# A hybrid decoder step: parameters, sample states and small state outputs cross memory channel-major instead of being transposed on the chip

## What is computed

```
u    = rmsnorm(x, norm_g);  proj = u @ w_in          # 8704 columns
lx, lg, sb, scg, sh, sg, q, qg, mg = split(proj)
# A: conv of width 4 over lx (buffer: 3 old inputs), gated linear recurrence from h0
xc, new_lru_buf = causal_dwconv(lx, lru_buf, lru_conv_w);  xc = xc + lru_conv_b
hs, new_h = rglru(xc, lru_h, lru_wa, lru_ba, lru_wx, lru_bx, lru_lambda)
z_a = (hs * silu(lg)) @ lru_wo
# B: conv of width 3 over scg * sh (buffer: 2 old inputs)
cy, new_sc_buf = causal_dwconv(scg * sh, sc_buf, sconv_w)
z_b = (silu(sg) * sb * cy) @ sconv_wo
# C: 4 heads of attention into 256 memory tokens
z_c = (attention(q, mem_k, mem_v) * silu(qg)) @ xa_wo
y = x + (sigmoid(mg_a) * z_a + sigmoid(mg_b) * z_b + sigmoid(mg_c) * z_c) @ w_out
```

## Time and profile before

| | |
|---|---|
| median of 3 runs | 780.32 us (775.95 to 801.77) |
| the profiled execution | 778.57 us |
| its spans, eight cores | 770.2 to 777.0 us |
| its granted clock, eight cores | 0.985 to 0.997 |
| span of the slowest core (core 4) | 777.0 us |
| PE busy on it | 727.6 us (94%) |
| DVE, ACT, POOL busy on it | 398.3, 344.8, 246.0 us |

### The profile page before, as it was taken

How to read it: one execution, slowest core, us unless ns; L and a number is a source line. 1 busy time by engine, 2 the same in 40 slices (tenths; PEclk the granted TensorE clock), 3 DMA queues, 4 the chain that set the end, 5 groups by cost and what they waited for, 6 DMA issues and landing times.

```text
span 777.0 us, 13244 instructions; the slowest of 8 cores (770.2 to 777.0 us)
## 1 busy us (share of the span) xinstructions
PE 727.6 (94%) x4884; PEld 459.4 (59%) x4884; DVE 398.3 (51%) x379; ACT 344.8 (44%) x408; POOL 246.0 (32%) x303
## 2 busy tenths in 40 slices
PE   2887999989999989989999999999999999999995
PEld 1555656556566546646666656666666666665442
DVE  3444253747849529727975865546321221223675
ACT  4346378687694776777661211121211112112332
POOL 5555101202103002102023344435464554523211
PEclk9999999999999989989999999999999999999998
DMA  9998934422613322412333694655895848226833
GB/s 201 187 191 148 135 72 40 41 24 19 54 17 35 34 26 28 41 11 29 38 38 72 96 182 80 101 112 65 112 111 68 109 55 74 26 109 217 288 149 139
DMA packets 112618, 69.47 MB, mean 89 GB/s; under 512 B 93987, under 2 KB 100213, under 8 KB 112539
## 3 DMA queue, kind: packets, MB, share of 16 engines
q0 software_dynamic: 99808, 31.60, 40.3%
q1 hardware_dynamic: 12747, 37.03, 14.4%
HBM read 90.53 MB, written 9.82 MB: 129 GB/s over the span
## 4 chain that ended last, share of the span: by engine, by line
PE 84%; DMA 6%; ACT 3%; DVE 2%; issue 2%; POOL 1%; POOLq 0%; SPq 0%; ACTq 0%; DVEq 0%
PE PP L644 72%; PE PP L1211 8%; DMA R<-xp 3%; DMA R<-w_in 3%; PE PP L989 2%; ACT R L847 1%; PE PP L981 1%; DVE R L834 1%; PE PP L1075 1%; ACT R L984 1%; PE PP L1114 0%; POOL R L692 0%; POOL R L702 0%; ACT R L698 0%; PE PP L770 0%
## 5 line engine op out<-in xcount | busy, mean ns | idle before, releaser
L644 PE MATMUL PP<-R 128*128 128x344 bf16 x4104 | 619.7, 311 | 7.7 <-ACT R L847 4.0
L644 PEld LDWEIGHTS PP<-R 128*128 128x128 bf16 x4104 | 399.4, 98 | 216.1 <-issue 19.4
L1163 ACT ACTIVATE R<-PP 128x688 f32<-128x688 f32 x72 | 53.5, 743 | 221.1 <-PE PP L644 188.3
L134 POOL DMA_DIRECT2D R<-w_in x68 | 61.5, 905 | 276.6 <-PE PP L644 265.3
L1172 DVE SCALAR_TENSOR_TENSOR R<-R,PP 128x688 f32<-128x688 f32 x72 | 62.6, 871 | 151.1 <-PE PP L644 137.0
L1211 PE MATMUL PP<-R 128*128 128x512 bf16 (+1 forms) x272 | 59.0, 379 | 0.0
L1176 POOL TENSOR_TENSOR R<-R 128x688 f32<-128x688 f32 x24 | 39.4, 1641 | 36.8 <-DVE R L1172 35.9
L1211 PEld LDWEIGHTS PP<-R 128*128 128x128 bf16 (+1 forms) x272 | 26.4, 97 | 32.3 <-issue 0.4
L834 DVE SCALAR_TENSOR_TENSOR R<-R 128x2048 f32<-128x2048 f32 x18 | 42.3, 2349 | 5.4 <-ACT R L831 4.4
L1181 POOL TENSOR_TENSOR R<-R 128x688 bf16<-128x688 f32 x24 | 39.0, 1641 | 18.4 <-DVE R L1172 18.0
L1220 ACT ACTIVATE R<-R 128x1024 f32<-128x1024 f32 (+1 forms) x17 | 18.0, 1057 | 46.3 <-DVE R L1215 46.3
(11 more groups left out here) (131 smaller groups left out, 592.5 us busy)
## 6 DMA issues: line engine op xcount, KB each, us to landing
R<-w_in POOLq DMA_DIRECT2D x68, 256.0 KB, 5.9
R<-xp SPq DMA_DIRECT2D x32, 512.0 KB, 6.1
R<-ck SPq DMA_DIRECT2D x16, 512.0 KB, 4.4
y_p<-R SPq DMA_DIRECT2D x16, 512.0 KB, 2.9
R<-cv POOLq DMA_DIRECT2D x16, 256.0 KB, 7.4
R<-w_out POOLq DMA_DIRECT2D x8, 256.0 KB, 7.9
R<-xa_wo POOLq DMA_DIRECT2D x14, 128.0 KB, 4.9
R<-lru_wo POOLq DMA_DIRECT2D x8, 192.0 KB, 4.0
```

Source lines behind the costliest of these rows:

```text
L134: eng.dma_start(out=out, in_=in_).then_inc(sems[semkey], 16)
L644: return lambda e: e.matmul(ps.ap[:, b * 512:b * 512 + BLK], lhs(k), rhs[:, k, c:c + BLK], start=(k == 0), stop=(k == nk - 1))
L1163: G.act(lambda e, ps=pg[u], th_=th_: e.activation(out=b3(th_.ap), in_=pv(ps), func=AF.Tanh, scale=0.5), UW, [pg[u].tok], [th_.tok], Px - E ...
```

## The change

The parameters come as one tensor of 128 x 82, the samples' states as one of 128 x 576, and the small state outputs leave as one of 128 x 324: all with the channel within its block as the first axis. The rearranging is done where the inputs are prepared and the outputs gathered. All else stays, the reads and writes of `pT`, `SIT` and `SO` too.

```diff
+    st_T = din("st_T", [128, 36 * TS])
+    par = din("par", [128, 82])
...
+    o_T = dout("o_T", [128, NCH * 54])
+    o_lc = dout("o_lc", [TS, 2 * W])
+    o_sc = dout("o_sc", [TS, W])
...
-        G.dma("sp", [(prg[0:8, :], norm_g.rearrange("(r c) -> r c", c=128)), (prg[8:16, :], mem_norm_g.rearrange("(r c) -> r c", c=128))],
-              8192, [], [m_prg.t], -190, "prg")
-        h = Handle(PS)
-        G.pe([lambda e, h=h: e.transpose(h.ap[:, 0:16], prg, ident[0:16, 0:16])], 0.1, [m_prg.t, m_ident.t], [h.tok], -150)
-        G.dve(lambda e, h=h: e.tensor_copy(pT[:, 0:16], h.ap[:, 0:16]), 16, [h.tok], [t_pg], -150)
-
-        def params():
...
-            G.dma("sp", [(prt[r0:r0 + nr, :], v.rearrange(pat, c=128) if pat else v.rearrange("(r c) -> r c", c=128))
-                         for v, r0, nr, pat in plist], 42000, [], [m_prt.t], 20, "prt")
-            G.after(G.tasks[-1], t_xd[10])
-            h = Handle(PS)
-            G.pe([lambda e: e.transpose(h.ap[:, 0:66], prt, ident[0:66, 0:66])], 0.3, [m_prt.t, m_ident.t], [h.tok], 30)
-            G.dve(lambda e: e.tensor_copy(pT[:, 16:82], h.ap[:, 0:66]), 66, [h.tok], [m_pT.t], 30)
+        dsem("par")
+        G.dma("sp", [(pT, par[:, :])], 42000, [], [m_pT.t], -190, "par")
...
-                [ps.tok, t_pg], [tdst], prio)
+                [ps.tok, m_pT.t], [tdst], prio)
...
-        params()
-        m_sin = Mem("sin", m_xc.off, 4608, F32)
-        t = G.dma("sp", [(sin[0:TS, 0:2304], st_lc[:, :]), (sin[0:TS, 2304:3072], st_h[:, :]),
-                      (sin[0:TS, 3072:4608], st_sc[:, :])], 300000, [], [m_sin.t], 25, "sin")
+        t = G.dma("sp", [(m_SIT.ap, st_T[:, :])], 294912, [], [m_SIT.t], 25, "sin")
         G.after(t, t_xd[15])
...
-        t = G.dma("sp", [(o_slc3[:, 0:2, :], st_lc3[:, 1:3, :]), (o_ssc3[:, 0:1, :], st_sc3[:, 1:2, :])], 150000,
-                  [], [t_dram[0]], 30, "out")
+        t = G.dma("sp", [(o_lc[:, :], st_lc[:, W:3 * W]), (o_sc[:, :], st_sc[:, W:2 * W])], 150000, [], [t_dram[0]], 30, "out")
         G.after(t, t_rs[18])
...
-            G.pe([trs(gi) for gi in range(18)], 1.8, [m_sin.t, m_ident.t], [h.tok], 42)
-        G.dve(lambda e, h=h: e.tensor_copy(
-            SIT.rearrange("p (g a) b -> p g (a b)", g=2),
-            h.ap.rearrange("p (g c) -> p g c", g=2)[:, :, 0:18 * TS]), 576, [h.tok], [m_SIT.t], 42)
...
-        m_sot = side("sot", 20480, W, F32)
...
-        G.pe([trso(n) for n in range(NCH)], 1.0, [t_SO, m_ident.t], [pss.tok], PM + 30)
-        G.dve(lambda e: e.tensor_copy(so_tok[0:54, :].rearrange("p (g c) -> p g c", g=2),
-                                      pss.ap.rearrange("p (g c) -> p g c", g=2)[0:54, :, 0:384]), 768, [pss.tok], [m_sot.t], PM + 30)
-        G.dma("sp", [(o_plc[:, :], so_tok[0:3, :]), (o_ph[:, :], so_tok[3:4, :]), (o_psc[:, :], so_tok[4:6, :]),
-                     (o_slc3[:, 2, :], so_tok[6:22, :]), (o_sh[:, :], so_tok[22:38, :]), (o_ssc3[:, 1, :], so_tok[38:54, :])], 200000,
-              [m_sot.t], [t_dram[3]], PM + 30, "out")
+        G.dma("sp", [(o_T[:, :], m_SO.ap)], 165888, [t_SO], [t_dram[3]], PM + 30, "out")
```

More of the change, by code:

```diff
@@ L741, in build_program @@
             p0(17 + i, memp[i * 128:(i + 1) * 128, :], 128, mnT[:, :, i * 128:(i + 1) * 128], pT[:, 8:16], t_mn[i], -80 + i, w_toks[-1:])
-        params()
-        m_sin = Mem("sin", m_xc.off, 4608, F32)
-        sin = m_sin.ap
         for k in ("sin", "out"):
             dsem(k)
-        t = G.dma("sp", [(sin[0:TS, 0:2304], st_lc[:, :]), (sin[0:TS, 2304:3072], st_h[:, :]),
-                      (sin[0:TS, 3072:4608], st_sc[:, :])], 300000, [], [m_sin.t], 25, "sin")
+        t = G.dma("sp", [(m_SIT.ap, st_T[:, :])], 294912, [], [m_SIT.t], 25, "sin")
         G.after(t, t_xd[15])
[L753 to L756, removed]
         t_dram = [Tok(f"dram{i}") for i in range(8)]
-        t = G.dma("sp", [(o_slc3[:, 0:2, :], st_lc3[:, 1:3, :]), (o_ssc3[:, 0:1, :], st_sc3[:, 1:2, :])], 150000,
-                  [], [t_dram[0]], 30, "out")
+        t = G.dma("sp", [(o_lc[:, :], st_lc[:, W:3 * W]), (o_sc[:, :], st_sc[:, W:2 * W])], 150000, [], [t_dram[0]], 30, "out")
         G.after(t, t_rs[18])
[L761 to L770, removed]
-            G.pe([trs(gi) for gi in range(18)], 1.8, [m_sin.t, m_ident.t], [h.tok], 42)
-        G.dve(lambda e, h=h: e.tensor_copy(
-            SIT.rearrange("p (g a) b -> p g (a b)", g=2),
-            h.ap.rearrange("p (g c) -> p g c", g=2)[:, :, 0:18 * TS]), 576, [h.tok], [m_SIT.t], 42)
         def bc(c0):
@@ L1249 @@
     shared = {
-        "norm_g": f(norm_g[0]), "mem_norm_g": f(mem_norm_g[0]), "w_in": f(w_in[0]),
-        "lru_conv_w": f(lru_conv_w[0]), "lru_conv_b": f(lru_conv_b[0]), "lru_wa": f(lru_wa[0]),
-        "lru_ba": f(lru_ba[0]), "lru_wx": f(lru_wx[0]), "lru_bx": f(lru_bx[0]), "lru_lambda": f(lru_lambda[0]),
-        "lru_wo": f(lru_wo[0]), "sconv_w": f(sconv_w[0]), "sconv_wo": f(sconv_wo[0]), "xa_wk": f(xa_wk[0]),
+        "par": f(np.concatenate([np.asarray(a).reshape(-1, 128) for a in (
+            norm_g[0], mem_norm_g[0], lru_conv_w[0], lru_conv_b[0], lru_ba[0], lru_bx[0], lru_lambda[0], sconv_w[0])]).T),
+        "w_in": f(w_in[0]),
+        "lru_wa": f(lru_wa[0]),
+        "lru_wx": f(lru_wx[0]),
+        "lru_wo": f(lru_wo[0]), "sconv_wo": f(sconv_wo[0]), "xa_wk": f(xa_wk[0]),
         "xa_wv": f(xa_wv[0]), "xa_wo": f(xa_wo[0]), "w_out": f(w_out[0]), "final_norm_g": f(final_norm_g),
@@ L1264 @@
         m["cv"] = f(np.asarray(cache_mem_v)[0, sl].reshape(TS, NM, XW))
-        m["st_h"] = f(np.asarray(state_lru_h)[0, sl])
+        st = np.concatenate([np.asarray(state_lru_conv)[0, sl].reshape(TS, 3, W), np.asarray(state_lru_h)[0, sl].reshape(TS, 1, W),
+                             np.asarray(state_sconv)[0, sl].reshape(TS, 2, W)], axis=1)
+        m["st_T"] = f(st.reshape(TS, 6, NCH, 128).transpose(3, 2, 1, 0)).reshape(128, 36 * TS)
         m["st_lc"] = f(np.asarray(state_lru_conv)[0, sl].reshape(TS, 3 * W))
@@ L1276 @@
     p_mv = np.stack([np.asarray(r["o_pv"]) for r in rs], axis=0).reshape(1, NCORES, NM, 4, 128).astype(np.float32)
-    p_h = cat("o_ph").reshape(1, NCORES, W).astype(np.float32)
-    p_lc = np.stack([np.asarray(r["o_plc"]) for r in rs], axis=0).reshape(1, NCORES, 3, W).astype(np.float32)
-    p_sc = np.stack([np.asarray(r["o_psc"]) for r in rs], axis=0).reshape(1, NCORES, 2, W).astype(np.float32)
-    s_h = cat("o_sh").reshape(1, NCORES * TS, W).astype(np.float32)
-    s_lc = cat("o_slc").reshape(1, NCORES * TS, 3, W).astype(np.float32)
-    s_sc = cat("o_ssc").reshape(1, NCORES * TS, 2, W).astype(np.float32)
+    ot = np.stack([np.asarray(r["o_T"]).reshape(128, NCH, 54).transpose(2, 1, 0).reshape(54, W) for r in rs], axis=0).astype(np.float32)
+    p_lc, p_h, p_sc = ot[None, :, 0:3], ot[None, :, 3], ot[None, :, 4:6]
+    s_h = ot[:, 22:38].reshape(1, NCORES * TS, W)
+    s_lc = np.concatenate([cat("o_lc").reshape(NCORES * TS, 2, W), ot[:, 6:22].reshape(NCORES * TS, 1, W)], axis=1)[None].astype(np.float32)
+    s_sc = np.concatenate([cat("o_sc").reshape(NCORES * TS, 1, W), ot[:, 38:54].reshape(NCORES * TS, 1, W)], axis=1)[None].astype(np.float32)
     return (y_prompt, y_sample, p_mk, p_mv, p_h, p_lc, p_sc, s_h, s_lc, s_sc)
```

17 lines of the change are left out of this document (removed).

## The result

Median after 770.68 us, before on the same chip 779.05; ratio 0.990, 95% interval 0.985 to 0.9949. A second comparison, with more runs, gave 770.73 against 778.36, ratio 0.9902 (0.9879 to 0.9924). The medians are over all executions, the ratios over those in which no die ran slower at a lower clock. By the bound of 2% that is no change; the interval shows that it is a gain of about 1%, some 8 us. The forecast was 773, in a range from 764 to 782.

A forecast was written before the change was run, and what follows sets the result against it. PE was taken as the bound, busy 94% of the span, with loads setting the pace before 66.85 us. 2.44 + 1.70 + 0.65 + 0.84 = 5.63 us off 778.57 gave 772.9, say 773, range 764 to 782.

The forecast's parts named there:

- The states' transposes: In the front where PE sets the pace, removing 36 transposes takes 2.44 us off PE.
- the fall of the clock: Behind the states' transposes, the clock dip on core 4 and other dipping cores goes: 1.70 us, bounds 0 and 1.70.
- What is late next: Memory keys and values: PE arrives 4.14 us earlier, the values' weights are there 0.7 us before wanted, no new wait.
- rival (c): Front's gain hidden: values' weights or last tiles late, 4.14 us become a wait; 777.1 us, chance 0.18.
- The states' load: Load issued some 12 us earlier, into the stretch that loads bound: counted 0, between -1.5 and 5.1 us.
- The small outputs: Start of the merge: six transposes gone, 0.65 us, and PE's wait for a PSUM tile gone, 0.84 us.
- The parameters: Front's first microseconds: one load replaces two loads, a transpose and a copy, and four later ACT table loads go: 0.
- The half of 196 GB/s: Assumed rate for the parameters' load in 328-byte rows: 0.4 us instead of 0.2, swallowed by 2.4 us to spare.
- the lower end that I named: First square on ACT starts up to 0.9 us earlier, if it can use the table that Ln leaves.
- Both ends of the start: First square on ACT 0.9 us earlier to 0.6 later; leads into the stretch that loads bound, counted 0.
- (b): Rival: a new order makes the last two attention heads like the first, 7.6 us better; 765.3 us, chance 0.15.
- (a): Rival: a new order makes the first two attention heads like the last two, 7.6 us worse; 780.5 us, chance 0.17.

The follow-up runs named there:

- t1: Changed kernel with 2 transposes of 16 columns put back on PE, in two tasks planned at 1.8 us each: 772.18 us, ratio to before 0.9923.
- late_load: Changed kernel with the states' load put back behind the last square, orders of PE, ACT and POOL unchanged: 771.05 us, ratio to before 0.9905.
- late_notab: late_exp with its order kept, but Exp and Ln issued at the first two squares and copies in their late places: 774.81 us, ratio to before 0.9959.
- p_outs: Kernel before with only the small outputs changed (stored channel-major, no transposes of them): 776.39 us, ratio to before 0.9963.
- t36: Changed kernel with all 36 state transposes put back on PE, results unused, planned duration as in t1: 774.52 us, ratio to before 0.9936.
- late_exp: Changed kernel with the parameters' Exp and Ln planned behind the 16th token tile's inverse root: 774.28 us, ratio to before 0.9953; repeated as late_exp_b, 774.56 us.

## Why the prediction was right, and where it wasn't

**The states' transposes, 2.44 us of PE, and the fall of the clock, 1.70 on the cores that had it.** Right in kind, and the upper bound was right to take for core 4: the falls went on all five cores, come back with the transposes and not with dense work of the same length. In size the sum is somewhat high: 36 transposes put back cost 2.2 us where it gives 2.9. The Trainium skill ("TensorE: Matmul & The Clock Gate", Part 4: PE-mode transpose), that transposes don't engage the full clock as matmuls do, agrees in its direction. That every core pays, as I worked it out from that rule, it did not: 16 of 32 did with 36 transposes, and all of eight only with 72.

**What is late next: nothing, 0.7 us to spare.** Right that there is no new wait: PE idles for 0.01 us between 70 and 100 us on the mean core, and rival (c), the hidden gain, fell. The margin was wider than 0.7: the values' weights landed some 3 us before the keys were done. In the changed kernel 16 other matmuls stand between; in t1 the values follow the keys at once (94.2 and 97.6 us on the mean core), and PE doesn't wait there either.

**The states' load: 0.** Right, by late_load, for the four microseconds that could be tried.

**The small outputs, 0.65 + 0.84 = 1.49.** Right: -1.6 in that stretch in the changed kernel, -1.5 with this part alone. The SP and POOL steps behind it cost nothing that shows.

**The parameters: 0.** This is the term that was mis-sized: alone the part gains 3.3 us (1.9 to 4.5). The load itself was in time: at 3.04 us, and with Exp and Ln done ACT still waited 1.22 us for the first tile. (The Trainium skill, "DMA: Bandwidth & Descriptors", Specifications, puts transfers below 512 bytes under line rate; 1.9 us for 41 KB neither shows nor excludes that, and here nothing hung on it. The half of 196 GB/s that I put in for it is a guess that no run shows.) Of its working, one half was right: the table loads on ACT that go between 65 and 97 us are worth nothing (late_notab), and the first square starts earlier, by 0.6 us on the mean core and 0.9 between the slowest ones. That this meets the lower end that I named is luck: I had two table loads in it, and with one it is the arrival of the tile that sets the start. "Both ends of the start lead into a stretch that loads bound; I take 0 there too" was short by up to 0.7 us, little beside that stretch's own scatter. What was left out is the order. I had written that the scheduler may interleave the rest otherwise with ACT's tables in another state, but as a rival of either sign, not as a price of this part.

**The states' order, which hid that error.** The three kernels without transposes and with late Exp gain only 115.3 - 113.1 = 2.2 us from the 200th to the 800th matmul, where I had 3.5 for the mean core. Their loss from 70 to 180 us is no smaller than before (5.4 to 5.6 against 5.2), though the clock lost between 70 and 100 us fell from 1.2 to at most 0.4: idle time elsewhere took its place, among it 1.05 us between 100 and 120, where before there were 0.41, and falls of the clock between 160 and 180 us (0.4 to 0.6 us), where before there were none. So one new order takes about 1.3 us away, and the early Exp gives about 2.1 back. The 1.3 are a difference, not a measurement: with p_outs as the base, which has the order of before there (114.5), they would be 2.1, and with the transposes at what t36 showed instead of the sum, some 0.7 less. Both orders were priced at nothing, and that the sum came out near is in part luck: their signs differ.

**Rivals.** (b), the heads get better, hardly came: PE's idle time from 140 to 180 us on the mean core went from 3.4 to 1.1 and 1.7 us in the two profiles after, but from 100 to 140 it grew from 0.4 to 2.4 and 1.8. The heads around 270 and 330 have six falls of the clock on the eight cores instead of nine, but p_outs, with the order of before, has five. The third and fourth heads did not become like the first. (a), the heads get worse, is what late_exp's order does in a small way around the first head.

## What to carry to other kernels

Where a scheduler orders the work by its own estimates, removing instructions also reorders the rest; what the removed instructions cost themselves was summed to within 1 us here (2.9 for 2.2, 1.49 for 1.5), and the reordering was worth 1 to 2 us of either sign on top. To find out which of the two a gain comes from, put the removed instructions back with the planned duration unchanged, or keep the order and take the instructions out. And a small instruction with its operands there early can be worth planning early, as Exp and Ln were here, not for its own time but for what it leaves to the plan behind it.

## What the hardware showed that I had not expected

36 transposes of 16 columns, 2.5 us of PE (in the kernel before and in p_outs with one small matmul between the two lots), were followed by a fall of the granted clock to its lower level on half of the cores (16 of 32), 72 on all (8 of 8); 17 matmuls of the same length on none. Within a kernel the order on PE was the same on all cores; what makes a core one of the half, the runs don't tell.

Exp and Ln of a few columns, one right behind the other, took one table load (at 3.04); with a Silu between them, as before and in late_exp_b, they took one each, and the Silus that followed another.

A load of 41 KB in rows of 328 bytes was there 1.9 us after its issue, at 3.04 us from the start; the two vectors of before, 4 KB each and issued one behind the other, had been there at 3.24.
